# Expert-matrix step of a two-block kernel: one-hot rows per token by tensor_scalar, and 32 early units instead of 7

## The reference

```python
q = (xb @ w_q).reshape(tb, PEER_HEADS, 2, PEER_DKEY // 2)
s = jnp.einsum('thpd,hpnd->thpn', q, sub_keys)
sv, si = lax.top_k(s, k)                       # k = 16, of 128 keys, twice
cand = (sv[:, :, 0, :, None] + sv[:, :, 1, None, :]).reshape(tb, PEER_HEADS, k * k)
cand_idx = (si[:, :, 0, :, None] * PEER_NKEYS + si[:, :, 1, None, :]).reshape(tb, PEER_HEADS, k * k)
top_v, top_i = lax.top_k(cand, k)
experts = jnp.take_along_axis(cand_idx, top_i, axis=-1)
g = jax.nn.softmax(top_v, axis=-1)
a = jax.nn.gelu(jnp.einsum('td,thkd->thk', xb, u[experts]), approximate=False)
return jnp.einsum('thk,thkd->td', g * a, v[experts])
```

## Time and profile before

| | before |
|---|---|
| median of 3 runs | 1644.35 us |
| the runs | 1643.14 to 1644.89 us |
| profiled execution | 1643.05 us |
| its span, first to last instruction | 1641.2 us |
| around the span | 1.85 us |
| mean granted TensorE clock (share of 2.4 GHz) | 0.944 |

### The profile page before, as it was taken

The page is one execution under the profiler, slowest core; times in us unless marked ns, Lnnn a source line. Parts: engine busy times, 40 slices in busy tenths (PEclk is TensorE's granted clock), DMA queues, the critical chain, the costliest instruction groups (busy, mean ns, idle before and its releaser), DMA issues.

```text
span 1641.2 us, 21960 instructions
## 1 busy us (share of the span) xinstructions
PE 1452.2 (88%) x8980; PEld 1304.3 (79%) x8980; DVE 978.1 (60%) x1487; ACT 708.7 (43%) x991; POOL 558.9 (34%) x324
## 2 busy tenths in 40 slices
PE   6989887787998878788566699999999999999997
PEld 6878777687986656688555688899999999999996
DVE  4645666688656756499788855544444444444444
ACT  5545643233444334433323244544444444444442
POOL 2431122334353110476679822221221222212212
PEclk9999999899998979999778899999999999999999
DMA  6533275555665752534400046655555555565554
GB/s 209 158 105 92 85 263 183 175 193 179 193 211 188 249 180 74 190 112 130 139 4 1 1 141 198 211 188 191 182 192 188 186 192 185 188 190 184 191 188 171
DMA packets 185812, 265.75 MB, mean 162 GB/s; under 512 B 8000, under 2 KB 119360, under 8 KB 185456
## 3 DMA queue, kind: packets, MB, share of 16 engines
q1 hardware_dynamic: 181760, 249.93, 47.4%
q0 software_dynamic: 3376, 12.78, 2.3%
q10 hardware_dynamic: 576, 1.64, 0.3%
HBM read 259.86 MB, written 4.46 MB: 161 GB/s over the span
## 4 chain that ended last, share of the span: by engine, by line
PE 62%; DVE 17%; DMA 8%; POOL 6%; ACT 3%; issue 3%; SPq 1%; DVEq 0%; ACTq 0%; POOLq 0%
PE bank L596 18%; PE bank L627 15%; PE bank L601 9%; PE bank L632 8%; POOL sb_hot L2003 5%; PE bank L569 4%; DVE sb_ada_x L1503 3%; DMA sb_raw<-w_in 3%; PE bank L573 2%; DVE sb_lo L1246 2%; DMA sb_raw<-w_gate 2%; PE bank L892 2%; DMA sb_ada_w<-ada_w 2%; DVE sb_hot L1775 2%; DMA sb_raw<-w_down 1%
## 5 line engine op out<-in xcount | busy, mean ns | idle before, releaser
L1840 POOL TENSOR_TENSOR sb_lo<-sb_raw,sb_hi 128x1024 fp32r<-128x1024 f32 (+1 forms) x152 | 372.9, 2461 | 897.8 <-ACT sb_hi L924 897.8
L924 ACT ACTIVATE sb_hi<-sb_raw 128x1024 fp32r<-128x1024 f32 (+2 forms) x427 | 443.7, 1048 | 425.6 <-DMA sb_raw<-peer_v 126.1
L1246 DVE TENSOR_TENSOR sb_lo<-sb_raw,sb_hi 128x1024 fp32r<-128x1024 f32 (+2 forms) x276 | 360.5, 1311 | 403.9 <-ACT sb_hi L924 403.0
L596 PE MATMUL bank<-sb_act_hi,sb_hi 128*128 128x256 f32 x1632 | 411.5, 289 | 19.8 <-ACT sb_hi L924 19.5
L596 PE MATMUL bank<-sb_act_lo,sb_hi 128*128 128x256 f32 x1632 | 408.1, 287 | 0.0
L596 PEld LDWEIGHTS bank<-sb_act_hi,sb_hi 128*128 128x128 f32 x1632 | 319.6, 196 | 24.0 <-ACT sb_hi L924 20.7
L596 PEld LDWEIGHTS bank<-sb_act_lo,sb_hi 128*128 128x128 f32 x1632 | 319.7, 196 | 2.5
L601 PE MATMUL bank<-sb_act_hi,sb_lo 128*128 128x256 f32 x1632 | 234.3, 287 | 27.3 <-POOL sb_lo L1840 22.9
L627 PE MATMUL bank<-sb_hi,sb_hid_hi 128*128 128x512 f32 x600 | 236.5, 394 | 9.3 <-ACT sb_hi L924 9.3
L601 PEld LDWEIGHTS bank<-sb_act_hi,sb_lo 128*128 128x128 f32 x1632 | 214.1, 195 | 29.9 <-POOL sb_lo L1840 25.1
L627 PE MATMUL bank<-sb_hi,sb_hid_lo 128*128 128x512 f32 x600 | 236.1, 394 | 0.0
(11 more groups left out here) (320 smaller groups left out, 1519.9 us busy)
## 6 DMA issues: line engine op xcount, KB each, us to landing
sb_raw<-peer_uT SPq DMA_DIRECT2D x128, 512.0 KB, 3.7
sb_raw<-peer_v SPq DMA_DIRECT2D x128, 512.0 KB, 3.6
sb_raw<-w_in SPq DMA_DIRECT2D x52, 512.0 KB, 4.4
sb_ada_w<-ada_w SPq DMA_DIRECT2D x12, 1024.0 KB, 5.2
sb_ada_w<-ada_w POOLq DMA_DIRECT2D x12, 1024.0 KB, 6.1
sb_raw<-w_gate SPq DMA_DIRECT2D x22, 512.0 KB, 5.7
sb_raw<-w_up SPq DMA_DIRECT2D x22, 512.0 KB, 5.4
sb_raw<-w_down SPq DMA_DIRECT2D x22, 512.0 KB, 4.7
```

What stands on the lines that cost most here:

```text
L596: e.matmul(bank[:, j * T:(j + 1) * T], hi[:, k, j * P:(j + 1) * P], part[:, k0 + k, :], start=i == first_i and j == 0 and k == 0 and part ...
L924: e.activation(flat_of(i, "hi"), flat_of(i, "raw"), ACT.Copy).then_inc(hi_done[i % R], 1)
L1246: e.tensor_tensor(flat_of(i, "lo"), flat_of(i, "raw"), flat_of(i, "hi").bitcast(F32), ALU.subtract).then_inc(lo_done[i % R], 1)
L1840: e.tensor_tensor(flat_of(i, "lo"), flat_of(i, "raw"), flat_of(i, "hi").bitcast(F32), ALU.subtract).then_inc(lo_done[i % R], 1)
```

## The change

1. The one-hot matrices of a group are made by 8 `tensor_scalar` of 128 elements on DVE, two per token: `is_equal` against the first place, and `is_equal` then `mult` with the second place and the weight as per-partition scalars. POOL's L2003 is gone. There are two `hot` buffers instead of three.
2. 16 early units (32 blocks) are set between the 64 groups of the G stage, one block and then two groups, on every engine (`expert_matrix_order`). Their lo is on DVE alone (`early_G=0`). They use three more buffers for their Gelu and are stored like the others.
3. `SELECT_ORDER` has 16 E instead of 7, the first of them ahead of the last H. In all 32 units are early, so in the expert stage every second unit is one whose u part has been done.

```diff
-POOL_SHARE = dict(early=1, ctx_in2=1, w_gate=2, w_up=2, down=2, wq=1)
+POOL_SHARE = dict(early=1, early_G=0, ctx_in2=1, w_gate=2, w_up=2, down=2, wq=1)
-SELECT_ORDER = "HDHHDHDHHDHDHEDEDEEDEDEE"
+SELECT_ORDER = "HDHHDHHDHHEDHEEDEEEDEEEDEEEDEEDEE"
+EARLY_BESIDE_G = 16
-EARLY = SELECT_ORDER.count("E")
+EARLY_BESIDE_SELECT = SELECT_ORDER.count("E")
+EARLY = EARLY_BESIDE_SELECT + EARLY_BESIDE_G
+HOT_BUFS = 2
+def expert_matrix_order():
+    n_blocks, q = 2 * EARLY_BESIDE_G, 0
+    for b in range(n_blocks):
+        yield "u", EARLY_BESIDE_SELECT + b // 2, b % 2
+        while q * n_blocks < (b + 1) * N_G:
+            yield "G", q, 0
+            q += 1
...
 # TensorE
-            for q in range(N_G):
-                bank = take("G", q)
-                pe.wait_ge(*hot_done.at(q))
+            for what, n, b in expert_matrix_order():
+                if what == "u":
+                    if b == 0:
+                        early_panel = feature_panel(("uT", n), act_T, h2)
+                    next(early_panel, None)
+                else:
+                    bank, h = take("G", n), hot[n % HOT_BUFS]
+                    pe.wait_ge(*hot_done.at(n))
...
 # ScalarE
-            for q in range(N_G):
-                copy_out(Gv[:, :, q * TG:(q + 1) * TG], psum("G", q)[:, :].rearrange("p (t i) -> p i t", t=TG), "G", q)
+            for what, n, b in expert_matrix_order():
+                if what == "u":
+                    hi_until(("uT", n), b)
+                    if b == 1:
+                        early_out(n)
+                else:
+                    copy_out(Gv[:, :, n * TG:(n + 1) * TG], psum("G", n)[:, :].rearrange("p (t i) -> p i t", t=TG), "G", n)
...
 # VectorE
-                if q >= HID_BUFS:
-                    dve.wait_ge(*full("G", q - HID_BUFS))
-                e.tensor_tensor(hot[q % HID_BUFS], iota.unsqueeze(1).unsqueeze(1).to_broadcast([P, 2, TG, P]),
-                                pT[:, 0:2, toks].unsqueeze(3).to_broadcast([P, 2, TG, P]), ALU.is_equal).then_inc(*hot_eq.inc(q))
+            for what, n, b in expert_matrix_order():
+                if what == "u":
+                    lo_until(("uT", n), b)
+                else:
+                    h = hot[n % HOT_BUFS]
+                    if n >= HOT_BUFS:
+                        dve.wait_ge(*full("G", n - HOT_BUFS))
+                    for j in range(TG):
+                        t = n * TG + j
+                        e.tensor_scalar(h[:, 0, j, :], iota, pT[:, 0, t:t + 1], None, ALU.is_equal)
+                        ins = e.tensor_scalar(h[:, 1, j, :], iota, pT[:, 1, t:t + 1], pT[:, 2, t:t + 1], ALU.is_equal, ALU.mult)
+                    ins.then_inc(*hot_done.inc(n))
...
 # GpSimd
-            for q in range(N_G):
-                pool.wait_ge(*hot_eq.at(q))
-                h = hot[q % HID_BUFS][:, 1]
-                e.tensor_tensor(h, h, pT[:, 2, q * TG:(q + 1) * TG].unsqueeze(2).to_broadcast([P, TG, P]), ALU.mult).then_inc(*hot_done.inc(q))
...
 # SyncE
+            for what, n, b in expert_matrix_order():
+                if what == "u":
+                    load_until(("uT", n), b)
+                    if b == 1:
+                        store_early(n)
```

More of the change, by code:

```diff
@@ L295, in build @@
                 n_split += 1
-                share = POOL_SHARE.get("early" if b.key[0] == "uT" and b.key[1] < EARLY else b.key[0], 4)
-                lo_on_pool[i] = n_split % share == 0
+                kind = b.key[0]
+                if kind == "uT" and b.key[1] < EARLY:
+                    kind = "early" if b.key[1] < EARLY_BESIDE_SELECT else "early_G"
+                share = POOL_SHARE.get(kind, 4)
+                lo_on_pool[i] = share > 0 and n_split % share == 0
         def flat_of(i, what):
@@ L391, in build @@
         ada_in = [sem(f"ada{i}_in") for i in range(ADA_BUFS + ADA_LATE_BUFS)]
-        early_stored = [sem(f"early{i}_stored") for i in range(3)]
+        early_stored = [sem(f"early{i}_stored") for i in range(6)]
         hid_in = [sem(f"hid{i}_in") for i in range(HID_BUFS)]
@@ L491, in build @@
         pT = pick_T.rearrange("p (w t) -> p w t", w=3)
-        TG = 4
-        N_G = T // TG
-        hot = [place(f"hot{i}", 1024, F32, OFF["hid"] + 1024 * i).rearrange("p (w t n) -> p w t n", w=2, n=P) for i in range(HID_BUFS)]
+        hot = [place(f"hot{i}", 1024, F32, OFF["hid"] + 1024 * i).rearrange("p (w t n) -> p w t n", w=2, n=P) for i in range(HOT_BUFS)]
         end_i, end_g2_i, end_g_i = span["end_x",][0], span["end_g2",][0], span["end_g",][0]
@@ L887, in tensor_program @@
                 give("picks", t)
-            for q in range(N_G):
-                bank = take("G", q)
-                pe.wait_ge(*hot_done.at(q))
[L891 to L894, removed]
+            early_panel = None
+            for what, n, b in expert_matrix_order():
[7 more added lines that the diff above has]
+                    for j in range(TG):
+                        ins = e.matmul(bank[:, j * P:(j + 1) * P], h[:, 1, j, :], h[:, 0, j, :], start=True, stop=True)
+                    ins.then_inc(*fills("G", n))
+                    give("G", n)
             for b in range(4):
@@ L1176, in scalar_program, with early_out @@
             norm_out("peer", mcol["sc2"], mcol["sh2"], [mod_done.at("sc2")])
+            def early_out(u):
+                b, nth = early_slot(u)
+                act.wait_ge(early_stored[b], 16 * nth)
+                act.wait_ge(*full(("uT", u)))
+                e.activation(by_chunk(early_buf[b]), by_chunk(psum(("uT", u))[:, :]), ACT.Gelu).then_inc(*gives(("uT", u)))
             n_h = n_e = n_d = 0
@@ L1185, in scalar_program @@
                     hi_until(("uT", n_e))
[L1186 to L1189, removed]
+                    early_out(n_e)
                     n_e += 1
@@ L1210, in scalar_program @@
                             act.wait_ge(*hid_used["peer", at - HID_BUFS])
+                        elif at == 2:
+                            for b in (3, 4):
+                                act.wait_ge(early_stored[b], 16 * len(range(b - 3, EARLY_BESIDE_G, 3)))
                         act.wait_ge(*full(("uT", u)))
@@ L2079, in sync_program @@
                     load_until(("uT", n_e))
-                    sp.wait_ge(*freed(("uT", n_e)))
-                    e.dma_start(parked_units[n_e], early_buf[n_e % 3]).then_inc(early_stored[n_e % 3], 16)
+                    store_early(n_e)
                     n_e += 1
+            for what, n, b in expert_matrix_order():
+                if what == "u":
+                    load_until(("uT", n), b)
+                    if b == 1:
+                        store_early(n)
             sp.wait_ge(x_parked, 16)
```

28 lines of the change are left out of this document (21 added, 7 removed).

## The result

| | before | after |
|---|---|---|
| median | 1643.74 us | 1714.97 us |
| runs | 1642.12 to 1644.89 (4) | 1710.94 to 1718.49 (4) |
| profiled execution, span | 1641.2 us | 1713.9 us |
| select stage (first matmul to first one-hot row) | 141.0 us | 211.7 us |
| G stage (to the first matmul behind it) | 131.0 us | 272.4 us |

The changed kernel takes 1.0433 times as long (95% interval 1.0408 to 1.0459), 71 us more. 1708 was forecast.

A forecast was written before the change was run, and what follows sets the result against it. Two loops, not an engine's load, were taken to decide: an early unit's store-then-load loop and a chain through four engines in the G stage. Against 1644.35, +64 +144 -144 gave 1708 us, range 1655 to 1755.

The forecast's parts named there:

- expert stage: Last stage: 25 more early units each take 5.76 us off PE, -144.0 us, 687.8 to 543.8.
- select stage: Stage ahead of the G stage: more early units at about 8.2 us each, G stage starting at 886.4, +64 us.
- G stage: Stage of 64 groups with 16 early units set between: sixteen pairs of blocks at 17.2 us, 275 where 131, +144.
- The loop Gelu, store, load, rounding: Select and every second G-stage block: loads wait behind the store; an early unit costs about 8.2 us, PE 5.76.
- The step: Select, from one early unit to the next: 14 steps of 8.2 us each.
- The one with the Exp: Select, the one early-unit step with the Exp in between: 11.3 us, as in the trace before.
- The chain: G stage: copy, rounding, subtraction, one-hot rows and groups wait on each other through four engines, 7.25 us a block.
- The one-hot rows: G stage on DVE: 0.20 us per new instruction, eight of them 1.6 us a group.
- the clock: G stage: PE at 0.85, 30% of the time at 1.2 GHz, taking a pair from 15.75 to 17.2 us.
- Two signs of the prediction: G stage: PE busy for under two thirds, and ACT's roundings waiting for DMA at every second block.
- Rival B: G stage fills up: a pair costs PE's 10.3 us, the stage 164.5, the kernel 1597; chance 0.06.
- The rule on pipeline flushing: New one-hot instructions on DVE: by the rule 0.28 us each, the stage 21 us more, 1730 in all.

The follow-up runs named there:

- the string alone: The kernel before with only the changed kernel's SELECT_ORDER, 16 early units in select and none in the G stage; 1655.98 us against 1643.16, ratio 1.0073.
- the later subtraction: The changed kernel with VectorE making a block's lo two blocks ahead instead of three in the G stage; 1599.42 us against 1643.16 for the kernel before.
- the kernel with the stores later: The changed kernel with the next unit's two loads ahead of an early unit's store on SyncE's queue; 1656.01 us against 1642.20 for the kernel before.
- the kernel with the rows alone: The kernel before with eight tensor_scalar per group for the one-hot rows, no GpSimd multiply, three hot buffers; 1629.88 us against 1643.16, ratio 0.9913.

## Why the prediction was right

The direction, the size (+64 us median forecast, +71 measured) and the two causes hold. Term by term, from the profiled executions:

| term | forecast | measured | where |
|---|---|---|---|
| expert stage | -144.0 | -144.5 | after, by stage |
| select stage | +64 | +70.6 (after), +65.8 and +65.0 in two other kernels with the same string | stages of after, the string alone, the later subtraction |
| G stage | +144 | +141.4 | after, by stage |
| earlier stages | 0 | +5.1 in the profiled execution | varies from execution to execution |

**Select.** The loop Gelu, store, load, rounding sets it: moving the store alone takes 31 to 37 us off it (206.1 to 211.7 down to 174.6), and PE-bound steps of 5.8 us appear. The first Gelu came at 758.3, 753.4 forecast; 5 us of that are the late start. The step was sized a little small: 14 steps average 8.7 us, 8.2 forecast, 7 us in all. One is the step around the last head (10.3). Four others take 9.3 to 9.9 us instead of mostly 7.9 to 8.3, because 6.1 to 6.6 us pass from the load's issue to the rounding instead of mostly 4.4 to 5.1. Two of these have a D of the string in them and two come one step behind such a one; what slows the load there was not tried and stays open (some 1.5 us four times, 6 us). The one with the Exp was forecast at 11.3 and took 9.3: before, the Exp waited 5.8 us for VectorE's search, and now it doesn't wait. From the last Gelu to the first one-hot row it takes 8.6 us, and not "the same steps" as before, 6.84: the G stage's first subtraction stands ahead of that row and waits for a rounding, which waits for a load issued behind the last store. VectorE's row:

```profile
896.78 1.23 DVE L1287 TENSOR_TENSOR sb_lo<-sb_raw,sb_hi 128x1024 fp32r<-128x1024 f32 x1 [1.62 <-ACT sb_hi L953]
897.93 0.28 DVE L1821 TENSOR_SCALAR sb_hot<-sb_const,sb_pick_T 128x128 f32<-128x128 f32 x1
```

Where that subtraction isn't ahead, in the string alone and with the later subtraction, it takes 5.9.

**G stage.** The chain was laid out rightly: copy, rounding 0.49 us later, subtraction 1.09 later (1006.59 to 1007.68), 1.14 to the first one-hot row. Two sizes were off, and they nearly cancel, which is luck. The one-hot rows were put at 0.20 us each: true for the form with one scalar, but the second scalar and the second operation together cost another 0.06 us, so a group took 1.81 us and not 1.6, which at the high clock makes 16.15 us a pair where 15.75 was forecast (9.0 + 6.73 + 2 x 0.21). And the clock was 0.87, not 0.85, and cost less: 17.03 us a pair measured is 0.9 above that, where 1.45 had been added. The lower level acts in two places. The last group ahead of a u block comes after an idle PE, at a granted clock of 0.50, and takes 2.05 us instead of 1.13 (1021.33 to 1023.37 in the pair shown above). The u block's first sixteen matmuls take 2.29 us in that pair and 3.41 in the next one instead of 1.92, and with them the Gelu and the load behind it come later: in the next pair ScalarE waits 2.4 us for DMA and not 0.8. The first of these seems the larger part: the kernel with the stores later, where nothing waits for a load, takes 16.0 us a pair, 0.6 above the 15.3 of its chain at the high clock (2 x (7.25 + 0.42)).

Two signs of the prediction did not come. PE was busy for 70% of the stage (192 of 273 us), not for under two thirds. And ScalarE waited for DMA 9 times in 16 pairs, 12.6 us in all, not at every second block; in the other pairs the load had landed in time.

**Rival B** (the stage fills up) was said to decide below 13.2 us a pair and to need the rounding out of the chain. Each block's subtraction moved by one block does it, with the rounding left where it was: 10.4 us a pair. The price put on it, 10.3 a pair, was PE's 2.88 + 2 x 1.13 a block. That was the mis-sized term: 1.13 us is a group that stands alone, from its first start to its last end; back to back, groups cost less. 4.76 us a block less 2.88 for u leaves 0.94 a group. VectorE's own sum (1.14 + 2 x 1.81 = 4.76) is as large, so the stage is now full on both, and which of them would give way first wasn't tried.

**The rule on pipeline flushing.** The Trainium skill (VectorE: DVE Perf Modes, The DRAIN you can't avoid) says that the next operation does not start until the pipeline is empty, and adds that one that is not held back starts earlier. The prediction took the first half alone. By it each new instruction would have started when the one before ended, 0.28 us or 0.34 later; the rows show 0.20 and 0.26, some 0.09 sooner each, which agrees with the addition. The duration doesn't tell the distance: in the kernel with the rows alone the two forms last 0.33 and 0.40 us (medians) and start at the same 0.20 and 0.26.

The same page's advice to take tiles of 512 elements or more (section on the read-write bubble) was not refuted. The stage got 14 us shorter with eight instructions in place of one, but GpSimd's multiply, 1.97 us a group, had left it as well. VectorE's own time for a group went up, from 1.71 us on average beside GpSimd, and 1.21 for the shortest of them, to 1.81.

## What to carry to other kernels

When work of two kinds is woven into one fixed order on several engines, check for each wait what the awaited engine has in front of the awaited instruction: a lookahead counted in blocks is worth nothing where it ends in a row behind the very results that the waiting engine must produce. Each subtraction moved by one block was worth 109 us in the stages that it reaches, and the load of every engine was the same. And on a queue, what waits for a late result (a store) goes behind the loads that are already possible.

## What was not expected of the hardware

A second per-partition scalar with a second operation in `tensor_scalar` (128 elements, float32) costs 0.06 us from start to start (0.20 to 0.26) and 0.06 in duration (282 to 343 ns, medians of 256 each); which of the two costs it wasn't tried. A group of four 128 x 128 float32 products costs PE 1.13 us alone and about 0.94 among other matmuls. A 512 KB load behind a 256 KB store was rounded 4.4 to 5.5 us after its issue in twelve of the changed kernel's sixteen cases in select, and 6.1 to 6.6 us after it in the other four.
